# Moving the weights of the 512-column products to other byte offsets in SBUF

## The reference: what is computed

```python
for layer in range(DEPTH):                      # 2
    x = x + 0.5 * swiglu(rmsnorm(x, ...), gate, up, down)      # d_ff = 2816
    h = rmsnorm(x, ...)
    x = x + (conv_sparse_attn_mixer if layer % 2 == 0 else gated_deltanet_mixer)(h, ...)
    x = x + 0.5 * swiglu(rmsnorm(x, ...), gate, up, down)
return rmsnorm(x, final_gain)
```

## The kernel before, in words

| buffer | used by | bytes past a multiple of 256 |
|---|---|---|
| `plain_w[0]`, `plain_w[1]` | plain units, in turn | 0 and 0 |
| `wide[0]`, `wide[1]` | down, even m | 128 |
| `wide[2]` | down, odd m | 192 |
| `ab`, `a22`, `s12`, `s43` | fast pairs | 64 |

## Time and profile before

### The profile page before, as it was taken

How to read it: one execution, slowest core, us unless ns; L and a number is a source line. 1 busy time by engine, 2 the same in 40 slices (tenths; PEclk the granted TensorE clock), 3 DMA queues, 4 the chain that set the end, 5 groups by cost and what they waited for, 6 DMA issues and landing times.

```text
span 1996.9 us, 30677 instructions
## 1 busy us (share of the span) xinstructions
PE 1967.4 (99%) x12159; PEld 1733.6 (87%) x12159; DVE 1386.3 (69%) x1928; ACT 978.3 (49%) x1472; POOL 516.9 (26%) x530
## 2 busy tenths in 40 slices
PE   9999999999999999999999999999999999999998
PEld 7898998787788988998898999878888888989996
DVE  6964977588647955973894696376766558946963
ACT  5543653445645633653562464355564555524642
POOL 1201311454221301311130221157566111302311
PEclk9999999999999999999999999999999999999999
DMA  5232332444122232332233223222222122332331
GB/s 189 94 129 85 106 130 72 121 130 135 54 85 95 106 118 83 110 126 82 95 114 104 90 107 125 72 77 96 69 77 92 53 95 95 114 108 85 117 127 43
DMA packets 63167, 199.95 MB, mean 100 GB/s; under 512 B 12816, under 2 KB 14896, under 8 KB 63024
## 3 DMA queue, kind: packets, MB, share of 16 engines
q1 hardware_dynamic: 59616, 196.55, 29.2%
q10 hardware_dynamic: 3408, 1.44, 0.3%
HBM read 188.51 MB, written 2.38 MB: 96 GB/s over the span
## 4 chain that ended last, share of the span: by engine, by line
PE 87%; DVE 6%; ACT 3%; issue 2%; POOL 1%; DMA 1%; ACTq 0%; SPq 0%; DVEq 0%; POOLq 0%
PE prod L590 16%; PE prod L592 15%; PE prod L591 15%; PE misc L684 6%; PE misc L685 6%; PE misc L686 6%; PE prod L684 4%; PE prod L685 4%; PE prod L686 4%; PE misc L905 2%; DVE h_lo L1619 1%; ACT L1443 0%; ACT h_hi L1156 0%; PE misc L784 0%; PE prod L980 0%
## 5 line engine op out<-in xcount | busy, mean ns | idle before, releaser
L590 PE MATMUL prod<-h_hi,p_hi 128*128 128x512 f32 x728 | 300.6, 413 | 2.2 <-DVE p_lo L1503 1.3
L592 PE MATMUL prod<-h_hi,p_lo 128*128 128x512 f32 x728 | 285.3, 392 | 0.0
L591 PE MATMUL prod<-h_lo,p_hi 128*128 128x512 f32 x728 | 284.4, 391 | 0.0
L590 PE MATMUL prod<-a_hi,d_hi 128*128 128x512 f32 x693 | 273.3, 394 | 0.0
L591 PE MATMUL prod<-a_lo,d_hi 128*128 128x512 f32 x693 | 272.8, 394 | 0.0
L592 PE MATMUL prod<-a_hi,d_lo 128*128 128x512 f32 x693 | 272.6, 393 | 0.0
L1503 DVE TENSOR_TENSOR d_lo<-raw,d_hi 128x1408 fp32r<-128x1408 f32 x64 | 104.0, 1626 | 240.1 <-ACT d_hi L1070 240.0
L2100 POOL TENSOR_TENSOR s_f<-raw 128x512 f32<-128x512 f32 x70 | 94.4, 1348 | 675.0 <-DVE s_lo L1578 361.9
L1070 ACT ACTIVATE d_hi<-raw 128x1408 fp32r<-128x1408 f32 x64 | 88.4, 1381 | 227.1 <-PE prod L592 226.5
L1503 DVE TENSOR_TENSOR p_lo<-raw,p_hi 128x1024 fp32r<-128x1024 f32 x86 | 111.6, 1298 | 77.4 <-ACT p_hi L1070 77.1
L590 PEld LDWEIGHTS prod<-h_hi,p_hi 128*128 128x128 f32 x728 | 137.2, 188 | 31.0 <-issue 8.5
(11 more groups left out here) (371 smaller groups left out, 5267.7 us busy)
## 6 DMA issues: line engine op xcount, KB each, us to landing
raw<-in_w SPq DMA_DIRECT2D x252, 512.0 KB, 3.4
raw<-in_wd SPq DMA_DIRECT2D x64, 704.0 KB, 4.2
blk<-blocks SPq DMA_DIRECT2D x16, 256.0 KB
x<-in_x SPq DMA_DIRECT2D x8, 256.0 KB, 5.9
k_dup<-k_dup SPq DMA_DIRECT2D x8, 256.0 KB, 3.5
silu_g<-g_rows SPq DMA_DIRECT2D x7, 256.0 KB, 4.8
out<-y_out SPq DMA_DIRECT2D x12, 128.0 KB, 1.9
raw<-in_w SPq DMA_DIRECT2D x4, 256.0 KB, 6.0
```

Of the source, the lines that this page charges most:

```text
L590: pe.matmul(bank, wh, hi, start=k == 0, stop=False)
L591: pe.matmul(bank, wh, lo, start=False, stop=False)
L592: ins = pe.matmul(bank, wl, hi, start=False, stop=k == tiles_n - 1)
```

## The change

The buffers for the 512-column products move by some tens of bytes. The plain buffers go to 32 and 224 bytes past a multiple of 256. The down buffers of the even units go to 96, that of the odd units to 160. A fourth entry of `wide`, in the same place as the third, keeps the old 192 for the last unit (m = 7) of the first down half of every FFN. The fast products' buffers stay where they are, and no instruction is added, removed or moved.

```diff
         plain_w = [tuple(w_part(f"p_{part}{i}", at + 2 * QB * j, 2 * QUAD) for j, part in enumerate(("hi", "lo")))
-                 for i, at in enumerate((0, 14 * QB + ALIGN))]
+                 for i, at in enumerate((32, 14 * QB + 224))]
         wide = [tuple(w_part(f"d_{part}{i}", at + HALF * P * 4 * j, HALF * P) for j, part in enumerate(("hi", "lo")))
-                for i, at in enumerate((2 * W_SHIFT, 4 * QB + 2 * W_SHIFT, 14 * QB + 3 * W_SHIFT))]
+                for i, at in enumerate((96, 4 * QB + 96, 14 * QB + 160, 14 * QB + 3 * W_SHIFT))]
...
             if is_down(n):
+                if n == down_unit(f, 0, KT - 1):
+                    return wide[3]
                 return wide[2 if u % 2 else 1 - ab_place(f, FT - 1)]
```

## The result

The changed kernel takes 2013.13 us (median of 4, 2011.86 to 2015.06) against 1998.23 us of the kernel before beside it (median of 4). The ratio is 1.0076, 95% interval 1.0064 to 1.0088: 15 us slower, where 7 us faster was forecast and the range ended at 2003.5. Of the rivals it is C, plain products losing the floor, and the down products got dearer too.

What follows compares the result with a forecast made beforehand. TensorE, busy 99% of the span, was taken as the bound, through its start-to-start times. Down gains 7.3 us and all else 0: 1998.8 - 7.3 = 1991.5, 1991.4 for the runs' median; 8-in-10 range 1985.5 to 2003.5 us.

Steps and rivals of the forecast that it cites:

- C: Plain products lose their stall-free 226.7 ns: 2004.8 us, or 2017 with a stall on each; chance 0.16.
- What bounds the kernel: TensorE, busy 99% of the span; what counts is the time from one matmul's start to the next.
- Which value?: Down products at 96 and 160: took 1.1 ns each, the mean of a light stall pattern (2.2) and none (0).
- Down's term: 512-column down products: excess goes from 9.6 to 2.3 us, a gain of 7.3 us.
- The plain term: 2736 plain products at 32 and 224: no change taken, with 0 to +18 us possible undisturbed, -3.8 to +3.8 disturbed.
- The last unit at 192: Last down unit of each first half: only its entry can change its pattern, -0.3 to +0.6 us, taken as 0.
- The writers: ScalarE and VectorE writing to the new offsets: nothing beyond 0.1 ns an element, hidden in down units.
- B: Stream excess grows smoothly with the offset's distance from a multiple of 256: -0.9 to +0.5, 1998 us; chance 0.22.
- D: The address does nothing, down's excess has another source: time stays at 1998.7 us; chance 0.05.

Runs made afterwards that it cites:

- the last version: Kernel before with down at 0, the last unit of each first half at 160, plain 0, fast 64: 1989.91 us against 1998.19, ratio 0.9958.
- the sweep: Kernel giving each down unit and each mixer plain unit its own offset, 0 to 224 in steps of 32; products cost 0 to 7.6 ns over 226.67.
- plain alone: Kernel before with only the plain buffers moved, to 32 and 224; down stays at 128 and 192: ratio 1.0038, 7.6 us slower.
- down alone: Kernel before with only the down buffers moved, to 96, 160 and 192; plain stays at 0: ratio 1.0018, 3.6 us slower.
- four exits: Kernel before with down at 0, the first half's last unit at 224, 32, 160, 96 in FFN 0 to 3: 1992.9 us against 2000.35, single execution.

## Why the prediction was wrong, point by point

- **What bounds the kernel** was right. A ns on a product in a full stream is a ns of the kernel: the steps' 12.1 and 4.2 us on plain and down products, less 3.4 us elsewhere, mostly in longer steps and small products, are the span's 13.0, and the last version's 8.7 us less in down came out as 8.3 us of the runs' median (11.1 us between the two profiles, with 2.5 of it in longer plain steps and small products).
- **The step that failed is "Which value?"** No row had an offset between multiples of 64. I estimated from the paces in the earlier trace rows that 32 bytes move the meeting of the two streams by 7.1 ns, about one stall, and took from this that the shift would remove one. That they meet at all was my inference; no run shows it. The size of a step says nothing of its sign, as the text itself admitted, and the number went into the sum all the same: 1.1 ns for 96 and 160, measured 7.6 and 6.7. Down's term was -7.3 us and came out at +4.2. (The sum also gave the 1.1 to the 132 products that keep 192, about 0.1 us.) Of the bounds, the upper one was set to the heaviest pattern seen, one stall on each product, and 7.6, eight stalls on seven, lay beyond it.
- **The plain term** was put at 0 since 0 and 64 were at the floor and 32 lies between. But 64 was seen only with 256 columns, where another offset is free than at 512: at 512 columns 64 costs 6.8, at 256 it is 0 that costs 6.7. At 512 columns the rows had one free offset, 128 and 192 that both pay, and nothing nearer. That called for C as the likeliest case, not the third.
- **C** had the mechanism and its decision point right (measured 6.7 ns, over 4.1). Its price for the heavy pattern, 18 us, was too high as a sum: in the profile plain gives 9.7 us. About 200 of the 2736 products are followed by a longer step and hardly pay; the others already paid 4.0 us before, 2.4 of it in the second mixer; and the longer steps shrank by 2.4 us, for which no run shows a reason. The reading of the earlier trace rows was low in itself: from rounded starts it gave 13 ns for four steps in the delta rule, where all digits give 21. Even so the range stopped at the lighter part of C.
- **The last unit at 192** was priced at -0.3 to +0.6 us for its own 33 products. What such a unit can do is decide the pace of the 924 fast products behind it in the same FFN: 4.1 us an FFN, 16 us in all, when down at 0 shows it. It didn't show in the change, nor in the change without the fourth buffer. I had seen in the trace that a pattern depends on its entry, used it for down, and not asked it of the untouched stage that follows.
- **The writers** were put at nothing, and rightly: ScalarE's splits take 1056 and 1380 ns, VectorE's 1278 and 1627, against the earlier trace rows.
- **B** (smooth in the distance) and **D** (no effect) fell with the sweep. D's claim that an offset changes nothing does not hold here: 233.5 against 226.5 ns for the same weight buffers, by the moving operand's place alone, with a granted clock of 1.00 in both stretches of that profile. Whether it is the reads that collide, no run shows.

## What to carry to other kernels

Where TensorE streams `fp32r` products without a gap, the distance between the weights' and the moving operand's start, modulo 256 bytes, is worth over 3% (7.6 of 226.7 ns) at 512 columns and 6% (6.7 of 113.3) at 256. Modulo 256 is as these runs show it at the free place: with down at 0, the even units' buffers start at multiples of 2048 bytes and the odd units' 256 past one, and from m = 1 on all take 7.25 us for 32 steps. It should be measured at the width in question, since a free distance at one width is a dear one at another (0 costs nothing at 512 columns and 6.7 ns at 256, 64 costs 6.8 ns at 512 and can be free at 256). A kernel that gives each unit another offset measures all of them in one run, but only for the entries that its order makes. After any change to such a stream, look at the start-to-start times of the untouched stages behind it too.

## What the runs showed of the hardware that was not expected

- At 512 columns distance 0 costs nothing, 4 bytes 5.7 ns, 32 bytes 6.7 ns, 96 bytes 7.6 ns a product of 226.7. At 256 columns 0 costs 6.7 ns, 64 nothing or 4.4, 96, 128, 160 and 192 cost 4.0, 5.3, 6.7 and 4.4, of 113.3.
- At 512 columns 16, 240 and 252 bytes each show a free pattern and a dear one, 192 shows 2.2 and 6.7 ns, 128 shows 5.7 and 6.9.
- The patterns last. Fast pairs of 84 products stay in the dear one for all 11 pairs, 110 us. A down half between two stretches of pairs can end it (FFN 0 with plain alone goes from dear to cheap), but need not (the offset sweep's FFN 2 is dear on both sides).
- The first fast pairs of an FFN, entered after waits for other engines, are cheap in one profile and dear in another of nearly the same code: four or five pairs in FFN 0 with plain alone, down alone, without the fourth buffer, with down at 0 and the exit at 192, and with four exits, six in FFN 2 or 3 of three of these kernels, but one pair (0.37 us) in the full change and none in the kernel before or the last version. Such a stretch is worth up to 2.2 us and the two of one kernel 3.5, near the spread of 3.6 us of the kernel before; it was not tried whether they are its cause.
- What makes the stall of 6.67 ns, and why 0, is open. Most of the lasting costs fit whole pieces of it: 1.7, 2.2, 3.3, 4.4, 5.3, 5.7 and 7.6 ns are 1/4, 1/3, 1/2, 2/3, 4/5, 6/7 and 8/7 of 6.67. Nothing here shows where the two streams meet.
